# ScalarE's squares in the attention loop of a hybrid encoder layer: another place in the engine's order

## The chip, the cores and the metric

The kernel runs on one core of a Trainium2 chip. The metric is the device time of one execution in microseconds (us); three executions of the kernel before took 1003.96, 1005.08 and 1006.52 us, the median is 1005.08 us.

## The reference

One inference step of a one-layer hybrid encoder, all in f32, with 1024 prompt rows, 32 sample rows and a model width of 1024:

```
h = RMSNorm(x); z = h @ W_in          -> qA kA vA qB kB vB, heads of 64
mixer A: 8 query heads, 2 key heads, window of own chunk + 2 chunks of 64, sinks
mixer B: 8 heads, own chunk + 8 chunks, learned relative bias
x = x + W_out @ concat(RMSNorm_a(out_A), RMSNorm_b(out_B))
x = x + HierMoE(RMSNorm(x))           -> top 1 of 4 groups, then top 2 of 8 experts
```

Two norms matter here. RMSNorm_a and RMSNorm_b take the mean square over the 512 columns that each mixer gives for a row. The norm ahead of the mixture of experts takes the mean square over all 1024 columns of the row with its residual.

## The kernel before, in words

The rows lie in nine tiles of 128 (index t from 0 to 8; tile 7, `SAMPLE`, holds the sample rows, tile 8, `LAST`, the last prompt rows). There are three stages. The first (to about 295 us) projects and normalises all tiles. The second (to about 655 us) is the attention loop, with the output projection, the second norm and the router woven in. The third chooses experts and runs 24 steps over packed rows, with the expert weights streaming in from memory.

**The attention loop** is written out by hand for every engine: 75 iterations v, one pair of heads each (`units`; eight pairs to a tile, even v mixer A, odd v mixer B; iteration v = 8t + 2p + m). A unit u = 2v or 2v+1 is one head. Each engine runs its own list in this order, and semaphores tie the lists together:

- **TensorE** (line 1635 on): `transpose_probs(2v-2)` (L1499), `scores(v+1)` (L1484), `turn_rows(v)` (transposes of finished rows: L1623 for the mixers' outputs, L1534 for the second norm's), a piece of the output projection (`pe_pieces(2v)`, L1597; for tile 7 L1574 and L1581), `pair_back(v-3)` (L1529, which turns a pair's output back), `transpose_probs(2v-1)`, another piece, `values(v-2)` (L1516), router pieces (L1550, L1561). In iterations 1 to 14 `keep_busy` (L1384) adds matmuls whose result nobody reads; one f32 matmul shows as two records.
- **ScalarE** (L886 to L896): `pair_out(v-3)` (L808, copies the pair's output out of PSUM), `copy_pt(2v-2)` (L828, L831), `turned_out(v)` (L881), `probs(2v+2)` (L842, the exponents; L847 for the sinks of mixer A), `act_pieces(2v)`, `copy_pt(2v-1)`, `probs(2v+3)`, `act_pieces(2v+1)`, and at v = 10, 18, ..., 74 `squares_out(t)` with t = v // 8 - 1.
- **VectorE**: `copy_pt(2v-2)` (L1056), `biased(2v+2)` (L1140, adds mask or bias and takes the row minimum of the negated scores), pieces (`residual`, L1093; the second norm, L1118), `divide(v-3)` (L1068 to L1075), `copy_pt(2v-1)`, `biased(2v+3)`, at v = 11, 19, ... `norm_out(t)` (L1085), and router copies (L1102, L1107).

The names that the change and the prediction touch:

- `squares_out(t)` (L849) waits until all eight pairs of tile t are divided (`s_on`) and the norm of the tile before is made (`s_og`). It squares 512 columns twice (L854), and `rstd` (L722 Ln, L723 Exp) turns the two sums into reciprocal roots; `s_so` tells VectorE. `norm_out(t)` on VectorE waits for `s_so`, and `turn_rows` on TensorE, one iteration later for the first half of the row, waits for `s_og` of `norm_out`.
- `act_pieces(t, g)` (L859): at the step g = `squares` of a tile (given by `when(t)`) it waits for the residual (`s_x2`), squares 1024 columns (L867) and calls `rstd`; VectorE's second norm (L1118) waits for that. All these steps are odd, so they lie in `act_pieces(2v+1)`: v = 22, 30, 38, 46, 54, 61, 68 and 71 for tiles 0 to 7. For tile 7 at g = 11 and 13 (v = 69 and 70) it waits for the sample's part of the output projection (`s_pq`, L1574) and copies it out (L864).
- `probs(u)` waits for `biased(u)` (`s_sp`). TensorE transposes unit u one iteration or more later.
- `copy_pt` waits for the transposes of its unit; `turn_rows(v)` waits for ScalarE's `copy_pt(2v-2)`; `pair_back(v-3)` waits for `pair_out(v-3)`.
- SyncE loads experts 1 to 4 when the last pair is turned back (`s_ob`, set by L1529).

Of the kernel before, what the change touches and what calls it, by code (L numbers as in the profile page):

```python
# [59 lines left out]
SAMPLE, LAST = NT - 2, NT - 1  # L60
# [49 lines left out]
def build(nc, d, o):  # L110
    ctx = ExitStack()
    with ctx:
        def sem(name):
            return ctx.enter_context(nc.semaphore(name))
# [5 lines left out]
        def place(n, at=None):  # L120
            a = top[0] if at is None else at
            if at is None:
                top[0] += n
            assert a + n <= ARENA, (a, n)
            return arena[:, a:a + n]
# [20 lines left out]
        sso, rso = place(2), place(2)  # L146
# [25 lines left out]
        parts = xr[:, 1].rearrange("p (b c) -> p b c", b=2)  # L172
# [89 lines left out]
        def stored(e, c):  # L262
            at = weight_at(e, c)
            return arena[:, at:at + 512]
# [15 lines left out]
        def bank(n, a=0, b=512):  # L280
            return ps[:, n * 512 + a:n * 512 + b]
# [58 lines left out]
        s_on = sem("mixer_out_divided")  # L340
        s_so = sem("mixer_squares_summed")
        s_og = sem("mixer_out_normed")
# [82 lines left out]
        def unit_info(u):  # L425

            t, m, h = units[u]
            segs = tile_keys(TILE[t])[m]
            tiles, c = [], 0
            for col, n in segs:  # L430
                for k in range(0, n, P):
                    tiles.append((c + k, (col + k) // P, min(P, n - k)))
                c += n
            return t, m, h, segs, tiles, c

        def stat_at(m, h):

            return h // 4 * 8 + m * 4 + h % 4
# [38 lines left out]
        def pt_of(u):  # L477
            _, m, h = units[u]
            return (pt_a, pt_b)[m][:, h % 2]
# [8 lines left out]
        def pieces(do, u):  # L488

            for t in (u // 16 - 3, u // 16 - 2, u // 16 - 1):  # L490
                if 0 <= t < LAST:
                    do(t, u - 16 * (t + 1))
# [205 lines left out]
        def _(act):  # L698
# [17 lines left out]
            chain = Chain(act, s_act)  # L716
# [3 lines left out]
            def rstd(out, ms):  # L720

                chain.link(nc.scalar.activation(out, ms, ACT.Ln, bias=eps))  # L722
                return nc.scalar.activation(out, out, ACT.Exp, scale=-0.5)  # L723
# [86 lines left out]
            def copy_pt(u):  # L810

                if not 0 <= u < NU:
                    return
                _, _, _, _, tiles, _ = unit_info(u)
                cut = (len(tiles) + 1) // 2
                act.wait_ge(s_pt, u + 1)
                rest = tiles[cut:]
                if not rest:
                    act.sem_inc(s_pta, 1)
                    return  # L820
                if u >= 4:
                    act.wait_ge(s_pv[u % 2], u // 2 - 1)
                c0 = 0
                full = [x for x in rest if x[2] == P]
                ins = None
                if full:
                    c0 = len(full) * P
                    ins = nc.scalar.activation(pt_of(u)[:, cut * P:cut * P + c0], bank(5, 0, c0), ACT.Copy)  # L828
                if len(full) < len(rest):
                    n = rest[-1][2]  # L830
                    ins = nc.scalar.activation(pt_of(u)[0:n, cut * P + c0:cut * P + c0 + P], bank(5, c0, c0 + P)[0:n], ACT.Copy)  # L831
                ins.then_inc(s_pta, 1)

            def probs(u):

                if u >= NU:
                    return
                t, m, h, segs, tiles, width = unit_info(u)
                act.wait_ge(s_sp, u + 1)
                c = stat_at(m, h)  # L840
                shift = negm[:, t % 2, c:c + 1]
                nc.scalar.activation(sp[:, u % 4, 0:width], sp[:, u % 4, 0:width], ACT.Exp, scale=-1.0,  # L842
                                     bias=shift, accum_out=psum_e[:, t % 2, c:c + 1]).then_inc(s_p, 1)
                if m == 0:
                    if t >= 1:
                        act.wait_ge(s_on, u // 2 - 7)
                    nc.scalar.activation(esink[:, h:h + 1], sinks[:, h:h + 1], ACT.Exp, bias=shift).then_inc(s_es, 1)  # L847

            def squares_out(t):  # L849
                act.wait_ge(s_on, 8 * (t + 1))  # L850
                if t >= 1:
                    act.wait_ge(s_og, 2 * t)
                for m in range(2):
                    ins = nc.scalar.activation(junk[:, 512 * m:512 * m + 512], row[:, t, 512 * m:512 * m + 512], ACT.Square,  # L854
                                               scale=512 ** -0.5, accum_out=sso[:, m:m + 1])
                chain.link(ins)
                rstd(rso, sso).then_inc(s_so, 1)

            def act_pieces(t, g):  # L859
                if t == SAMPLE and g in (11, 13):  # L860
# [9 lines left out]
            def turned_out(v):  # L870

                turn = turn_of(v)
                if turn is None:
                    return
                kind, t, half = turn
                made, done = ((s_t1, s_ota), (s_t2, s_h2a))[kind]
                act.wait_ge(made, 2 * t + half + 1)
                if kind == 0 and half == 0 and t >= 2:
                    for r in range(2):
                        act.wait_ge(s_r[r], t - 1)  # L880
                nc.scalar.activation(turned[t % 2][:, 4 * half:4 * half + 4], bank(5).rearrange("p (g c) -> p g c", g=4),  # L881
                                     ACT.Copy).then_inc(done, 1)
# [3 lines left out]
            for v in range(NV + 3):  # L886
                pair_out(v - 3)
                copy_pt(2 * v - 2)
                turned_out(v)
                probs(2 * v + 2)  # L890
                pieces(act_pieces, 2 * v)
                copy_pt(2 * v - 1)
                probs(2 * v + 3)
                pieces(act_pieces, 2 * v + 1)
                if v % 8 == 2 and v >= 8:
                    squares_out(v // 8 - 1)  # L896
            def choice_exps(n):

                t0, t1 = ((0, EARLY), (EARLY, NT))[n]
# [3 lines left out]
            def second_exps(n):  # L903
# [2 lines left out]
                act.wait_ge(s_v12, n + 1)  # L906
                nc.scalar.activation(e12[:, t0:t1], e12[:, t0:t1], ACT.Exp).then_inc(s_v12e, 1)

            act.wait_ge(s_t1, 2 * LAST + 1)
            for r in range(2):  # L910
                act.wait_ge(s_r[r], LAST - 1)
# [462 lines left out]
        def _(pe):  # L1374
# [6 lines left out]
            def keep_busy(n, b=2):  # L1381

                for _ in range(n):
                    mm(bank(b, 0, P), ident, ident, start=True, stop=True)  # L1384
# [251 lines left out]
            for v in range(NV + 3):  # L1636
                if v == 1:
                    pe.wait_ge(s_tea, 2 + 2 * NT)
                    pe.wait_ge(s_tev, 2 + 2 * NT)
                transpose_probs(2 * v - 2)  # L1640
                scores(v + 1)
                turn_rows(v)
                pieces(pe_pieces, 2 * v)
                pair_back(v - 3)
                rows_turned(v)
                transpose_probs(2 * v - 1)
                pieces(pe_pieces, 2 * v + 1)
                values(v - 2)
                pieces(route_pieces, 2 * v)
                pieces(route_pieces, 2 * v + 1)  # L1650
                if 1 <= v < FIRST_OUT:
                    keep_busy(6 if v == 11 else 5 - v // 4, 6)
            turn_logits(SAMPLE)
            keep_busy(16)
            pe.wait_ge(s_og, 2 * NT)
# [1 line left out]
            for half in range(2):  # L1657
                for c in range(4):
                    k = 4 * half + c
                    ins = nc.tensor.transpose(bank(6 + half, c * P, c * P + P), row[:, LAST, k * P:k * P + P], ident)  # L1660
# [36 lines left out]
            for s in range(NT):  # L1697
                ins = mm(ps[:, NT * NE:NT * NE + NE], ones, mb[:, s], start=(s == 0), stop=(s == NT - 1))
# [3 lines left out]
            for n in range(4):  # L1702
                ins = mm(bank(1, 0, 2 * NSTEP), late_row[:, n], late_block[:, n].rearrange("p a c -> p (a c)"),
                         start=False, stop=(n == 3))
# [58 lines left out]
            for s in range(NSTEP):  # L1763
# [8 lines left out]
                if s == 22:  # L1772

                    pe.wait_ge(s_oin, 1)
                    for n in range(2 * NT):
                        ins = mm(bank(7, 0, 2 * NOVER), over_row[:, n], over_block[:, n].rearrange("p a c -> p (a c)"),
                                 start=(n == 0), stop=(n == 2 * NT - 1))
# [5 lines left out]
            with pe.If(nov > 0):  # L1783
                with pe.Fori(0, NOVER) as i:
                    with pe.If(i < nov):
                        pe.wait_ge(v_g, i * 16 + 16)
                        for g in range(8):
                            ins = nc.tensor.transpose(bank(2 + g // 4, g % 4 * P, g % 4 * P + P), xg[:, 0, g * P:g * P + P], ident)
# [4 lines left out]
                        for k in range(KD):  # L1793
                            ins = mm(bank(0), xgt[:, 0, k], stored(0, k * 512), start=(k == 0), stop=(k == KD - 1))
                        ins.then_inc(v_gu, 1)
                        pe.wait_ge(v_h, i + 1)
                        for f in range(2):
                            ins = nc.tensor.transpose(bank(4, f * P, f * P + P), hd[:, 0, f * P:f * P + P], ident)
# [4 lines left out]
                        for f in range(2):  # L1803
                            for n in range(2):
                                a = 2 * KD * FF + f * D + n * 512
                                ins = mm(bank(5 + n), hdt[:, 0, f], stored(0, a), start=(f == 0), stop=(f == 1))
# [100 lines left out]
```

## Time and profile before

| what | value |
|---|---|
| three executions, median (lowest, highest) | 1005.08 us (1003.96, 1006.52) |
| the profiled execution, its own time | 1007.59 us |
| span of its records | 1005.8 us |
| mean granted TensorE clock over the span | 0.987 |
| busy: TensorE, VectorE, ScalarE, GpSimd | 951.7, 375.1, 318.9, 88.3 us |

The profile's page gives busy time for each engine over the span and over 40 slices. The waits view adds up, for each line, how long its engine sat idle ahead of it and which line ended that. The timeline lists instructions in order of time with start, duration, engine, line, tiles, how many are merged, and in brackets the idle time before. The windows view gives busy time of all engines in a stretch with the granted TensorE clock (1.00 is full speed). PE is TensorE's matmul, PEld its weight load, DVE VectorE, ACT ScalarE, SP SyncE.

### The profile page before, as it was taken

To read this page: it belongs to the slowest core of one execution; us is meant where nothing else is said; L and a number is where in the kernel's file an instruction comes from. 1 tells how busy PE (TensorE), PEld (TensorE's weight loads), DVE (VectorE), ACT (ScalarE), POOL (GpSimd) and SP (SyncE) were. 2 spreads that over 40 slices of the span, in tenths; PEclk is the share of its full clock that TensorE was granted. 3 is DMA by queue.
4 is the path that set the end of the run, shared out by engine and by line. 5 is a ranking of instruction groups with operands and counts; after the bars stand their busy time and mean duration, and the time that the engine had idled before them with its cause. 6 is when DMAs were issued, how large, how long until landed. Compare 5 with 4: busy or idle time off the path is not lost. (4 is left out here: it accounts for less than half of the span.)

```text
span 1005.8 us, 16201 instructions
## 1 busy us (share of the span) xinstructions
PE 951.7 (95%) x6097; PEld 478.0 (48%) x6097; DVE 375.1 (37%) x1083; ACT 318.9 (32%) x937; POOL 88.3 (9%) x72
## 2 busy tenths in 40 slices
PE   6999999999989999999998998998999999999994
PEld 3454554455456545555555554568333333333341
DVE  0342334333365555555555445467311111111120
ACT  1211222122246555555556455411111111111110
POOL 1000000000030000000000000000122222222111
PEclk9999999999989999999999999899999999999998
DMA  8501111011057001101010140297899999999942
GB/s 342 214 27 41 42 42 42 0 42 42 1 209 259 1 22 43 64 1 64 1 64 22 43 189 22 85 387 305 318 370 390 390 379 393 391 393 386 375 121 29
DMA packets 35015, 164.64 MB, mean 164 GB/s; under 512 B 7872, under 2 KB 9952, under 8 KB 22016
## 3 DMA queue, kind: packets, MB, share of 16 engines
q1 hardware_dynamic: 24768, 134.92, 33.7%
q0 software_dynamic: 6912, 17.32, 6.9%
q10 hardware_dynamic: 3264, 11.44, 2.8%
q8 instruction: 47, 0.77, 0.3%
q14 instruction: 24, 0.20, 0.1%
HBM read 147.10 MB, written 24.41 MB: 171 GB/s over the span
## 5 line engine op out<-in xcount | busy, mean ns | idle before, releaser
L1397 PE MATMUL ps<-arena 128*128 128x512 f32 (+1 forms) x640 | 252.2, 554 | 8.6 <-DMA arena<-in_w_in 8.6
L1397 PEld LDWEIGHTS ps<-arena 128*128 128x128 f32 x640 | 121.4, 191 | 134.3 <-issue 129.5
L1730 PE MATMUL ps<-arena 128*32 128x512 f32 x1536 | 171.7, 598 | 0.8 <-ACT arena L931 0.8
L1597 PE MATMUL ps<-arena 128*128 128x512 f32 x224 | 114.7, 606 | 0.0
L842 ACT ACTIVATE arena<-arena 128x256 f32<-128x256 f32 (+6 forms) x144 | 83.8, 582 | 83.3 <-DVE arena L1140 82.0
L1730 PEld LDWEIGHTS ps<-arena 128*32 128x32 f32 x1536 | 47.8, 110 | 107.0 <-issue 105.9
L1140 DVE CUSTOM_DVE_ANT_0 arena<-ps,arena 128x256 f32<-128x256 f32 (+6 forms) x144 | 78.0, 543 | 31.2 <-PE ps L1484 30.8
L1748 PE MATMUL ps<-arena 128*32 128x512 f32 x768 | 87.0, 592 | 0.7 <-ACT arena L955 0.7
L1056 DVE COPY arena<-ps 128x128 f32<-128x128 f32 (+2 forms) x144 | 53.1, 369 | 63.1 <-PE ps L1499 62.6
L1499 PE MATMUL ps<-arena 128*128 128x128 f32 (+1 forms) x400 | 71.3, 283 | 4.0 <-ACT arena L881 1.6
L761 ACT ACTIVATE arena<-ps,arena 128x512 f32<-128x512 f32 (+1 forms) x36 | 24.8, 689 | 156.8 <-PE ps L1397 155.8
L1337 DVE SCALAR_TENSOR_TENSOR arena<-ps,arena 128x256 f32<-128x256 f32 x24 | 11.6, 485 | 165.8 <-ACT arena L947 165.8
L996 DVE TENSOR_TENSOR arena<-arena 128x640 f32<-128x640 f32 (+1 forms) x18 | 18.5, 1027 | 131.4 <-ACT arena L759 79.4
L1484 PE MATMUL ps<-arena 64*128 64x256 f32 (+4 forms) x384 | 62.4, 424 | 1.1 <-DVE arena L1140 1.1
L638 POOL DMA_INDIRECT arena<-h_rows,arena x24 | 25.1, 1047 | 423.6 <-DVE arena L1287 405.3
L1516 PEld LDWEIGHTS ps<-arena 128*64 128x64 f32 (+1 forms) x800 | 42.5, 136 | 40.8 <-DVE arena L1056 21.2
L1516 PE MATMUL ps<-arena 128*64 128x128 f32 (+1 forms) x800 | 61.2, 283 | 0.6 <-ACT arena L881 0.6
L947 ACT ACTIVATE arena<-ps 128x256 f32<-128x256 f32 x24 | 9.3, 387 | 160.2 <-PE ps L1730 160.2
L1499 PEld LDWEIGHTS ps<-arena 128*128 128x128 f32 (+1 forms) x400 | 43.7, 139 | 28.9 <-issue 16.0
L649 POOL DMA_INDIRECT out_y<-arena x24 | 38.0, 1584 | 215.6 <-issue 148.9
L1748 PEld LDWEIGHTS ps<-arena 128*32 128x32 f32 x768 | 25.1, 109 | 57.7 <-issue 56.8
L1384 PE MATMUL ps<-arena 128*128 128x128 f32 x324 | 43.1, 286 | 0.0
(170 smaller groups left out, 883.8 us busy)
## 6 DMA issues: line engine op xcount, KB each, us to landing
arena<-in_wexp SPq DMA_DIRECT2D x92, 1024.0 KB, 22.0
arena<-in_x SPq DMA_DIRECT2D x18, 512.0 KB, 4.3
arena<-in_w_in ACTq DMA_DIRECT2D x3, 2048.0 KB, 23.2
arena<-in_xT SPq DMA_DIRECT2D x9, 512.0 KB, 3.5
arena<-in_w_out SPq DMA_DIRECT2D x1, 4096.0 KB, 13.9
out_y<-arena SPq DMA_DIRECT2D x8, 512.0 KB, 2.7
h_rows<-arena SPq DMA_DIRECT2D x8, 512.0 KB, 2.9
arena<-in_wexp SPq DMA_DIRECT2D x8, 512.0 KB, 20.6
```

The source lines that it names most:

```text
L649: pool.indirect_dma_start(out=o["y"], out_offset=bass.IndirectOffsetOnAxis(ap=slot_token[:, s:s + 1], axis=0), in_=yb[:, (s + 1) % 2], in_ ...
L842: nc.scalar.activation(sp[:, u % 4, 0:width], sp[:, u % 4, 0:width], ACT.Exp, scale=-1.0, bias=shift, accum_out=psum_e[:, t % 2, c:c + 1]) ...
L1056: nc.vector.tensor_copy(pt_of(u)[:, 0:cut * P], bank(4, 0, cut * P)).then_inc(s_ptv, 1)
L1140: nc.vector.tensor_tensor_reduce(out=sp[:, u % 4, 0:width], in0=ps[:, at:at + width], in1=add, scale=-1.0, scalar=nsinks[:, h:h + 1] if m ...
L1384: mm(bank(b, 0, P), ident, ident, start=True, stop=True)
L1397: ins = mm(bank(Z_BANK[c], 0, CHUNK[c]), xt[:, j, k, :], w_in[:, a:a + CHUNK[c]], start=(k == 0), stop=(k == KD - 1))
L1484: ins = mm(ps[:, at:at + step], q, kt[:, col:col + step], start=True, stop=True)
L1499: ins = nc.tensor.transpose(dst[0:n], sp[:, u % 4, c:c + n], ident)
L1516: ins = mm(pv_ps[r * HD:(r + 1) * HD], kv, pt_of(2 * v + r)[0:n, i * P:i * P + P], start=(i == 0), stop=(i == len(tiles) - 1), tile_positi ...
L1597: ins = mm(bank(6), turned[t % 2][:, c], w_out[:, c, 512 * n:512 * n + 512], start=(c == 0), stop=(c == KD - 1))
L1730: ins = mm(bank(s % 2)[u:u + UNIT], xgt[:, s % 2, k, u:u + UNIT], stored(expert_of(s, q), k * 512), start=(k == 0), stop=(k == KD - 1), ti ...
L1748: ins = mm(bank(5 + n)[u:u + UNIT], hdt[:, s % 2, f, u:u + UNIT], stored(expert_of(s, q), a), start=(f == 0), stop=(f == 1), tile_position ...
```

## The change

`squares_out` gets a list of halves; the waits go with half 0, the reciprocal roots with half 1. For tiles 0 to 7 it leaves the end of iteration v = 8t + 10 and runs in iteration v = 8t + 11: half 0 ahead of `probs(2v+2)`, half 1 behind `copy_pt(2v-1)`. For tile 8 it stands after the loop, which is the place it had. `act_pieces(2v+1)` changes places with `probs(2v+3)` in every iteration. On TensorE, `keep_busy` at the end of iteration 11 makes 14 matmuls in place of 6.

```diff
-            def squares_out(t):
-                act.wait_ge(s_on, 8 * (t + 1))
-                if t >= 1:
-                    act.wait_ge(s_og, 2 * t)
-                for m in range(2):
+            def squares_out(t, parts):
+                if 0 in parts:
+                    act.wait_ge(s_on, 8 * (t + 1))
+                    if t >= 1:
+                        act.wait_ge(s_og, 2 * t)
+                for m in parts:
                     ins = nc.scalar.activation(junk[:, 512 * m:512 * m + 512], row[:, t, 512 * m:512 * m + 512], ACT.Square,
                                                scale=512 ** -0.5, accum_out=sso[:, m:m + 1])
-                chain.link(ins)
-                rstd(rso, sso).then_inc(s_so, 1)
+                if 1 in parts:
+                    chain.link(ins)
+                    rstd(rso, sso).then_inc(s_so, 1)
...
                 turned_out(v)
+                if v % 8 == 3 and v >= 8:
+                    squares_out(v // 8 - 1, (0,))
                 probs(2 * v + 2)
                 pieces(act_pieces, 2 * v)
                 copy_pt(2 * v - 1)
+                if v % 8 == 3 and v >= 8:
+                    squares_out(v // 8 - 1, (1,))
+                pieces(act_pieces, 2 * v + 1)
                 probs(2 * v + 3)
-                pieces(act_pieces, 2 * v + 1)
-                if v % 8 == 2 and v >= 8:
-                    squares_out(v // 8 - 1)
...
+            squares_out(LAST, (0, 1))
             act.wait_ge(s_t1, 2 * LAST + 1)
...
                 if 1 <= v < FIRST_OUT:
-                    keep_busy(6 if v == 11 else 5 - v // 4, 6)
+                    keep_busy(14 if v == 11 else 5 - v // 4, 6)
```

## Rows read from the trace of the kernel before

**Rows 1.** The page, busy time of each engine over the span

```profile
PE 951.7 (95%) x6097; PEld 478.0 (48%) x6097; DVE 375.1 (37%) x1083; ACT 318.9 (32%) x937; POOL 88.3 (9%) x72
```

**Rows 2.** Waits of TensorE from 320 to 655 us: total, times, longest (us)

```profile
PE ps L1529 <- ACT arena L808: 12.6, 14, 1.4
```

**Rows 3.** Timeline, iterations 34 to 36 (squares of tile 3): start, us, instruction

```profile
438.34 0.48 DVE L1140 CUSTOM_DVE_ANT_0 arena<-ps,arena 128x256 f32<-128x256 f32 x1
438.38 0.62 ACT L854 ACTIVATE arena<-arena 128x512 f32<-128x512 f32 x1
...
440.06 0.21 ACT L723 ACTIVATE arena<-arena 128x2 f32<-128x2 f32 x1
440.43 0.28 ACT L808 ACTIVATE arena<-ps 128x128 f32<-128x128 f32 x1 [0.16 <-issue]
...
440.76 0.33 PE L1529 MATMUL ps<-arena 128*128 128x128 f32 x1 [1.40 <-ACT arena L808]
...
441.46 0.28 ACT L828 ACTIVATE arena<-ps 128x128 f32<-128x128 f32 x1
...
442.37 1.41 DVE L1085 SCALAR_TENSOR_TENSOR arena<-arena 128x512 f32<-128x512 f32 x2
...
445.13 0.56 DVE L1056 COPY arena<-ps 128x384 f32<-128x384 f32 x1 [1.35 <-PE ps L1499]
```

**Rows 4.** Timeline, iterations 9 to 12 (squares of tile 0, keep_busy)

```profile
322.78 0.94 PE L1384 MATMUL ps<-arena 128*128 128x128 f32 x6
...
325.87 0.33 PE L1529 MATMUL ps<-arena 128*128 128x128 f32 x1 [1.30 <-ACT arena L808]
...
327.06 1.60 PE L1384 MATMUL ps<-arena 128*128 128x128 f32 x12
...
327.48 1.41 DVE L1085 SCALAR_TENSOR_TENSOR arena<-arena 128x512 f32<-128x512 f32 x2
...
329.44 0.66 PE L1623 MATMUL ps<-arena 128*128 128x128 f32 x4
```

**Rows 5.** Timeline, iterations 68 to 71 (residual squares of tile 6, sample's parts)

```profile
624.01 0.39 ACT L828 ACTIVATE arena<-ps 128x256 f32<-128x256 f32 x1
...
625.68 0.83 ACT L842 ACTIVATE arena<-arena 128x640 f32<-128x640 f32 x1 [1.28 <-DVE arena L1140]
...
626.51 1.04 ACT L867 ACTIVATE arena<-arena 128x1024 f32<-128x1024 f32 x1
...
628.00 0.20 ACT L723 ACTIVATE arena<-arena 128x1 f32<-128x1 f32 x1
...
628.60 1.11 PE L1623 MATMUL ps<-arena 128*128 128x128 f32 x4 [2.19 <-ACT arena L828]
...
631.02 3.64 PE L1574 MATMUL ps<-arena 128*32 128x512 f32 x16
...
640.38 1.93 PE L1574 MATMUL ps<-arena 128*32 128x512 f32 x16
...
641.97 0.83 ACT L842 ACTIVATE arena<-arena 128x640 f32<-128x640 f32 x1 [1.29 <-DVE arena L1140]
...
642.79 0.58 ACT L864 ACTIVATE arena<-ps 128x512 f32<-128x512 f32 x1
...
643.76 0.66 PE L1534 MATMUL ps<-arena 128*128 128x128 f32 x4 [0.49 <-ACT arena L828]
```

**Rows 6.** Windows: stretch, length, busy PE PEld DVE ACT POOL, PEclk, DMA share, GB/s

```profile
628.40:635.20 6.80, 6.13 (x29) 2.42 (x31) 2.25 (x7) 2.77 (x10) 0.00 (x0) 0.50 0.49 157
...
725.00:960.00 235.00, 235.00 (x2132) 81.97 (x2128) 37.47 (x60) 37.34 (x81) 51.68 (x39) 1.00 1.01 383
```

**Rows 7.** Timeline of SyncE's queue, 600 to 1005 us

```profile
654.25 288.83 SPq L562 DMA_DIRECT2D arena<-in_wexp  x97
```

**Rows 8.** Groups of ScalarE: count, busy us, mean ns, idle before

```profile
L717 ACT ACT_TABLE_LOAD x1 | 1.3, 1283 | 9.1 <-issue 9.1
L927 ACT ACT_TABLE_LOAD x1 | 1.3, 1283 | 0.0
```

## The prediction, made before the change was run

> **What bounds the kernel now.** I read the page first: TensorE is busy for 951.7 of 1005.8 us, ScalarE for 318.9 [rows 1]. So ScalarE's busy time as such can give nothing; the change moves work on ScalarE and can only pay where TensorE stands still for it. The waits view of the attention loop answers that: 14 times `pair_back` (L1529) found TensorE idle and was released by ScalarE's copy of the pair's output (L808), for 12.6 us in all [rows 2]. The timeline says which 14. Each time the copy stands right behind a set of squares: eight times behind those of the mixers' output (tiles 0 to 7), six times behind those of the residual row (tiles 0 to 5). The residual squares of tile 6 have their stall one line earlier, at the transposes of a finished row, and it is the longest of the loop, 2.19 us [rows 5].
>
> Tile 3 shows the pattern [rows 3]. ScalarE ends an exponent and at 438.38 begins two squares, logarithm and exponent, until 440.27 (440.06 + 0.21). Only then does the next iteration's L808 run, and L1529 starts after 1.40 us of idle TensorE. The squares are wanted by nobody so early: VectorE's norm (L1085) begins at 442.37, right behind its own earlier work, not behind the squares. The loop ends at 654.25, where SyncE, which waited for the last L1529, issues the expert weights [rows 7]. From 725 to 960 TensorE is busy without a gap and the DMA engines are full [rows 6], but both start from the loop's end, so what the loop saves should reach the end of the kernel.
>
> **The change, part by part.** No instruction of ScalarE is added or removed and no DMA is moved; SyncE's and GpSimd's queues are untouched.
>
> *Mixers' squares, tiles 1 to 7.* L808 and the copy behind it now run right after the exponent, so in tile 3 L808 would end near 438.7, before TensorE is ready for L1529 at 440.76 - 1.40 = 439.36: the stall goes whole. What is late next? Half 0 takes 0.62, and the exponent behind it, whose scores were ready at 438.82 (438.34 + 0.48), moves to about 439.4; its transposes come an iteration later. Half 1 stands behind the copy L828, which follows TensorE and so moves from 441.46 to about 440.06 and ends at 440.34. Half 1 with both small steps takes 0.62 + 0.65 (440.27 less 438.38 less two squares of 0.62): the roots are ready at about 441.6. VectorE's norm would be free to run at 442.37 - 1.40 = 440.97, so here is a new wait of 0.65 us. The norm then ends at 441.65 + 1.41 = 443.06. Queued behind it on VectorE is the copy L1056 of the next iteration, which waits for TensorE until 445.13 - 1.40 = 443.73. So 0.67 us of cover is left, and the new wait costs nothing; if the cover goes, every further tenth delays the next scores. The second exponent of the iteration, now behind the squares, starts about when it did; TensorE needs it an iteration later.
>
> *Residual squares, tiles 0 to 5.* They change places with an exponent that was waiting for VectorE anyway: at tile 6 the copy ahead ends at 624.40, and the exponent waits until 625.68, 1.28 us of idle ScalarE [rows 5]. The residual is added before that copy ends, so the added wait (`s_x2`), with the exponent and the whole next iteration queued behind it, should hold nothing. Squares and small steps take 628.20 - 626.51 = 1.69 us; 1.28 of that fills the idle time, 0.4 us pushes the exponent and L808. The six stalls were of the order of 1 us and L808 now comes 1.3 us earlier, so they go whole. The second norm on VectorE, which waited for these roots, gets them earlier too.
>
> The thirteen stalls of both kinds together: 12.6 - 1.30 (tile 0, next) = **11.3 us** gained.
>
> *Tile 0 and the fillers.* In iteration 11 the stall of 1.30 goes [rows 4]. Behind it stand 8 more filler matmuls, 16 records; 6 records take 0.94 and 12 take 1.60, so 0.11 each, **1.77 us** more. Next is L1623, the transposes of the row that VectorE's norm makes. The norm ended at 327.48 + 1.41 = 328.89; with the stall gone it could end 1.30 earlier, with a wait like tile 3's 0.65 later than that. With the fillers L1623 starts at 329.44 - 1.30 + 1.77 = 329.9, behind the norm in every case. So the fillers set the time and are not hidden: **0.47 us** lost. The bounds are 0.47 and, should they be hidden, a gain of 1.30.
>
> *Residual squares of tile 6.* L1623 waited for a copy behind L867 [rows 5]. With the squares ahead of the exponent that copy comes earlier by the 1.28 us of idle time that they fill, less some 0.2 for handing over between instructions (an estimate; one such gap is 0.16 in [rows 3]). So of 2.19 us about 1.1 stays: **1.1 us** gained; bounds 0.9 and 2.19.
>
> *The sample's parts.* `act_pieces` at v = 69 and 70 also hold L864, which waits for L1574, and an exponent is now queued behind it. At v = 69 the scores' copies come later than that exponent, no cost. At v = 70 L1574 ends at 642.31; L864 (0.58) and then the exponent (0.83) end near 643.8, where they ended at 643.37. Next is the copy that L1534 already waited 0.49 us for [rows 5]. **0.5 us** lost, bounds 0 and 0.83.
>
> *The clock.* From 628.4 to 635.2 the granted clock is 0.50, its 1.2 GHz level [rows 6]; TensorE had just stood idle for 2.19 us. L1574 takes 3.64 us there and 1.93 at 640.38 [rows 5], 1.71 more; L1623 takes 1.11 against 0.66 [rows 4], 0.45 more. That is 2.2 us at least; half of the 6.13 us busy in that stretch, 3.1, is the upper bound; nothing, if the clock falls all the same. Idle spells up to 1.40 us [rows 3] left the clock at full speed, and the 2.19 becomes 1.1. I take the step as gone, **2.6 us**, between the two bounds.
>
> **Sum.** -11.3 + 0.5 - 1.1 + 0.5 - 2.6 = **-14.0 us**. The profiled execution took 1007.59 us with a span of 1005.8, so its like would be 993.6. It lies 2.5 us over the median of the three runs; from that median I predict 1005.1 - 14.0 = **991.1 us**.
>
> **Rivals.**
> - *The clock still falls* there or at a neighbour: around 1.1 us of idle the transposes and their copies leave TensorE lightly loaded, which speaks for it; the calm at 1.40 us speaks against it. Then 991.1 + 2.6 = 993.7.
> - *VectorE's norm takes the place of ScalarE's squares.* The cover is 0.67 us in tile 3. If the roots came more than that later than I work out, the next scores would wait. Should all eight sites give back what they gain, the six residual stalls remain, at the mean of 12.6 / 14 = 0.9 each 5.4 us; with 1.1, 2.6, -0.5 and -1.8 for the fillers that is 6.8: 998.3. Against it: the terms are single rows of a regular loop.
> - *Hidden behind the experts.* If the weights' stream set the end from a fixed time, 1005. Against it: 97 loads are issued from 654.25 on, after the loop's last step.
> - *Slower: ScalarE reloads its tables.* Squares now stand between exponents at more places. If a square needed another table than the exponent, each of eight sites would gain one more switch there and one back, 16 loads of 1.283 us [rows 8] = 20.5 us on the engine that TensorE waits for; from 0.9 us a load on, the 14 us are eaten. 991.1 + 20.5 = 1011.6. Against it: the trace has only two loads, one at the start and one ahead of the experts [rows 8], though exponents, squares and logarithms alternate all through the loop. The Trainium skill (ScalarE: Activation LUTs, Table sets: the hidden batching unit) has the rule behind this: batch activations by table set, not by place. Its section What ACT_TABLE_LOAD costs puts a switch at 2.66 us, an estimate of 42.6 us here, 1033.7; the load alone agrees with the 1.283 us of the rows, and no switch in the loop shows.
>
> **How the numbers follow.** Forecast 0.64; clock falls 0.20; norm's wait 0.08; hidden 0.05; slower 0.03 (tables, or a stall I did not see). The ends: with the whole 2.19, 3.1 for the clock, no loss at the sample and none for the fillers the sum is -11.3 - 1.3 - 2.2 - 3.1 = -17.9, 987.2; upward the range reaches past the clock's and the norm's case to 998.5, leaving out the last two cases. Runs of this kernel tell 0.3%, 3 us, from no change. Faster by more: the first three cases, 0.92; within: 0.05; slower: 0.03.
>
> **What would show it.** L1529 behind L808: from 14 stalls to none or short ones. ScalarE's wait for L1140 ahead of the exponents shrinks. VectorE shows a new wait of some 0.6 us for L723 ahead of L1085, and L1056 behind it still waits for TensorE. L1384 in iteration 11 has 28 records, and L1623 follows them later than before by half a microsecond relative to the copy ahead. Near 617 us the clock stays at 1.00 and L1574 takes 1.93 twice. SyncE's L562 starts near 640. The prediction is wrong if L562 moves and the end doesn't, if L1623 or L1484 take over the stalls, or if a stretch at 0.50 stands elsewhere.

## The result, and the profile after the change

The kernel with the change took 988.5 us (median of four executions, 988.11 to 990.68), the kernel before beside it 1005.28 us (four, 1003.96 to 1006.52). The ratio is 0.9838, 95% interval 0.9818 to 0.9857: 16.8 us faster, where 14.0 was forecast (991.1, range 987.2 to 998.5). The profiled execution took 988.11 us with a span of 986.3. Measured once more beside nine other executions of the kernel before, the change gave 0.9818 (0.9805 to 0.9832; run a1_again, below).

Page of the kernel after: busy time by engine, to set against [rows 1].

```profile
PE 946.2 (96%) x6113; PEld 480.9 (49%) x6113; DVE 375.0 (38%) x1083; ACT 317.4 (32%) x937; POOL 88.2 (9%) x72
```

ScalarE is as busy as it was; TensorE has 16 records more (the eight fillers) and yet the span is 19.5 us shorter. Waits of TensorE in the attention loop (318 to 640 us), all whose total is 1.0 us or more: line that waited, line that released it, total, times, longest.

```profile
PE ps L1504 <- ACT arena L883: 1.7, 3, 0.6
PE ps L1489 <- DVE arena L1145: 1.1, 4, 0.3
PE ps L1504 <- DVE arena L1061: 1.1, 2, 0.5
PE ps L1539 <- ACT arena L828: 1.1, 1, 1.1
PE ps L1628 <- ACT arena L828: 1.0, 2, 0.8
```

The lines moved by 5 below the edit: `pair_back` L1529 is now L1534, the transposes L1623 and L1534 are L1628 and L1539, VectorE's norm L1085 is L1090. The row of [rows 2] (12.6 us, 14 times) is gone, and no row of its size has come in. SyncE's queue shows the end of the loop, 18.83 us earlier than in [rows 7]:

```profile
635.42 290.19 SPq L562 DMA_DIRECT2D arena<-in_wexp  x97
```

Timeline of the tile 3 site, the stretch of [rows 3]:

```profile
433.58 1.13 PE L1602 MATMUL ps<-arena 128*128 128x512 f32 x2
...
433.73 0.26 ACT L808 ACTIVATE arena<-ps 128x128 f32<-128x128 f32 x1
...
434.04 0.63 ACT L855 ACTIVATE arena<-arena 128x512 f32<-128x512 f32 x1
...
434.12 0.14 PEld L1534 LDWEIGHTS ps<-arena 128*128 128x128 f32 x1 [0.24 <-ACT arena L808]
...
434.55 0.27 PE L1534 MATMUL ps<-arena 128*128 128x128 f32 x1
...
434.66 0.38 PE L1504 MATMUL ps<-arena 128*128 128x128 f32 x2
...
435.49 0.62 ACT L855 ACTIVATE arena<-arena 128x512 f32<-128x512 f32 x1
...
436.56 0.21 ACT L723 ACTIVATE arena<-arena 128x2 f32<-128x2 f32 x1
...
436.81 1.42 DVE L1090 SCALAR_TENSOR_TENSOR arena<-arena 128x512 f32<-128x512 f32 x2 [0.75 <-ACT arena L723]
...
438.74 0.56 DVE L1061 COPY arena<-ps 128x384 f32<-128x384 f32 x1 [0.52 <-PE ps L1504]
...
439.91 0.42 PEld L1628 LDWEIGHTS ps<-arena 128*128 128x128 f32 x4
439.91 0.66 PE L1628 MATMUL ps<-arena 128*128 128x128 f32 x4
```

The copy of the pair's output (L808) now precedes the two halves of the squares (L855). Its consumer's weights are loaded at 434.12, while the matmul ahead still runs, and L1534 starts without idle time. The norm (L1090) waits 0.75 us for the roots; the copy queued behind it (L1061) still waits 0.52 us for TensorE, so that wait is covered. The norm ends at 436.81 + 1.42 = 438.23, and L1628, TensorE's transposes of the row that the norm makes, starts 1.68 us later without idle time. VectorE's wait for the roots, summed over the loop:

```profile
DVE arena L1090 <- ACT arena L723: 5.5, 8, 1.0
```

These are eight waits of 0.5 to 1.0 us, one for each of tiles 0 to 7, and TensorE's list above has no wait for the norm (L1090). The wait of the second norm for its roots (8.8 us, 7 times before) is gone. Next come two stretches of TensorE: iterations 11 and 12 [rows 4] with 28 filler records, and tile 6 with the sample's parts [rows 5].

```profile
325.66 3.39 PE L1389 MATMUL ps<-arena 128*128 128x128 f32 x28
...
329.84 0.66 PE L1628 MATMUL ps<-arena 128*128 128x128 f32 x4
...
611.88 0.66 PE L1628 MATMUL ps<-arena 128*128 128x128 f32 x4 [0.78 <-ACT arena L828]
...
613.60 1.93 PE L1579 MATMUL ps<-arena 128*32 128x512 f32 x16
...
620.98 1.92 PE L1579 MATMUL ps<-arena 128*32 128x512 f32 x16
...
624.93 0.66 PE L1539 MATMUL ps<-arena 128*128 128x128 f32 x4 [1.07 <-ACT arena L828]
```

The stall of tile 6 fell from 2.19 to 0.78 us and the two passes of the sample's projection take 1.93 and 1.92. The sample's later stall grew from 0.49 to 1.07. The window from 600 us to the loop's end has the full clock, where [rows 6] had 0.50:

```profile
600.00:640.00 40.00, 34.44 (x300) 22.24 (x297) 21.42 (x63) 22.33 (x66) 0.00 (x0) 1.00 0.27 97
```

**Where the time came from.** The start of each `pair_back` in the kernel before, taken from its start after, tells how much earlier (minus) or later the kernel with the change is there. The table shows by how much this difference grows in each stretch. Worked out from the two traces' rows (us):

```
up to iteration 10                              +0.10
iteration 11  stall of tile 0                   -1.38   (reported idle 1.30)
iteration 12  fillers                           +1.66   forecast of both: +0.47, found +0.28
12 to 68      13 stalls                        -15.54   forecast -11.3
66            (no stall reported there)         -0.16
69, 70        tile 6 and the half clock         -4.09   forecast -1.1 - 2.6 = -3.7
71            sample's parts                    +0.58   forecast +0.5
sum                                            -18.83
one site (tile 3): iteration 35 -1.56, iteration 36 -0.18; reported idle 1.40
```

### The profile page after: what moved, and what is told of

The parts are those of the page before. It is cut to its first block and busy times, and to the rows that moved or that the text cites. A ratio compares the mean times of both kernels' runs of the same rounds, so it can differ in the third digit from the quotient of the medians.

```text
span 986.3 us, 16233 instructions
## 1 busy us (share of the span) xinstructions
PE 946.2 (96%) x6113; PEld 480.9 (49%) x6113; DVE 375.0 (38%) x1083; ACT 317.4 (32%) x937; POOL 88.2 (9%) x72
## 5 line engine op out<-in xcount | busy, mean ns | idle before, releaser
L1602 PE MATMUL ps<-arena 128*128 128x512 f32 x224 | 114.7, 606 | 0.0
L1061 DVE COPY arena<-ps 128x128 f32<-128x128 f32 (+2 forms) x144 | 53.1, 368 | 57.3 <-PE ps L1504 56.9
L1504 PE MATMUL ps<-arena 128*128 128x128 f32 (+1 forms) x400 | 70.6, 281 | 4.1 <-ACT arena L883 1.7
L1489 PE MATMUL ps<-arena 64*128 64x256 f32 (+4 forms) x384 | 62.4, 424 | 1.1 <-DVE arena L1145 1.1
L1504 PEld LDWEIGHTS ps<-arena 128*128 128x128 f32 (+1 forms) x400 | 44.2, 139 | 30.3 <-issue 18.5
L1389 PE MATMUL ps<-arena 128*128 128x128 f32 x340 | 46.5, 292 | 0.0
```

Of the source, the lines that this page charges most:

```text
L1061: nc.vector.tensor_copy(pt_of(u)[:, 0:cut * P], bank(4, 0, cut * P)).then_inc(s_ptv, 1)
L1489: ins = mm(ps[:, at:at + step], q, kt[:, col:col + step], start=True, stop=True)
L1504: ins = nc.tensor.transpose(dst[0:n], sp[:, u % 4, c:c + n], ident)
L1602: ins = mm(bank(6), turned[t % 2][:, c], w_out[:, c, 512 * n:512 * n + 512], start=(c == 0), stop=(c == KD - 1))
```

## The experiments

The theory (A in most expectations): TensorE lost what ScalarE's squares put between an exponent and the copies behind it; each stall is worth more than its reported idle time; the longest one also halved the clock. Rivals: the stalls are worth only their idle time (B, and the rest came from the clock or from chance); only one of the two moves matters; the halves, the fillers or the cover behind VectorE's norm are what makes it work.

**e1_mixers: the mixers' squares alone.** The swap of the residual squares is undone.

```diff
-                pieces(act_pieces, 2 * v + 1)
                 probs(2 * v + 3)
+                pieces(act_pieces, 2 * v + 1)
```

> The mixers' squares moved in halves, with 14 fillers in iteration 11; the residual squares stay behind the exponent. Theory A (a stall of TensorE costs its reported idle time and about 0.34 us more, because the instructions behind it start with nothing loaded ahead): seven sites 5.98 + 7 x 0.34 = 8.4 us gained, fillers 0.3 lost, so SyncE's expert loads start at 654.25 - 8.1 = 646.1; the half-clock stretch behind iteration 68 stays. Time about 997.2. Theory B (a stall costs its reported idle time, and the rest of what the changed kernel gained has another source, such as VectorE's later norm): 5.98 - 0.3 = 5.7 us, loads at 648.5, time about 999.6.

Measured: 998.15 us (996.7 to 999.1, four executions), ratio 0.9925 (0.9909 to 0.9942); the loads begin at 646.25. Waits and timeline of TensorE, and a window (length, busy PE, PEld, DVE, ACT, POOL, granted clock, DMA share, GB/s):

```profile
PE ps L1534 <- ACT arena L808: 5.3, 6, 1.1
...
621.13 1.11 PE L1628 MATMUL ps<-arena 128*128 128x128 f32 x4 [2.19 <-ACT arena L828]
...
619.70:626.50 6.80, 4.89 (x23) 1.82 (x23) 2.41 (x7) 3.65 (x14) 0.00 (x0) 0.50 0.43 154
```

Six stalls are back, and with the 2.19 us of tile 6 so is the stretch at half clock. The mixers' sites step as in the kernel after (tile 3: -1.56 and -0.18), so the two moves are independent. In this execution the clock was also halved for 3.4 us at 544.6 us, 0.4 us after the 1.03 us stall of iteration 55, and `pair_back` lost 1.69 there; the kernel after shows nothing there.

**e2_residual: the residual squares alone.** The kernel before, with the swap only.

```diff
-                probs(2 * v + 3)
                 pieces(act_pieces, 2 * v + 1)
+                probs(2 * v + 3)
```

> The residual squares change places with the exponent, the mixers' squares stay where they were, 6 fillers in iteration 11. Theory A: six sites 5.32 + 6 x 0.34 = 7.4 us, tile 6 and the clock 4.1, the sample's parts 0.6 lost: loads start at 654.25 - 10.9 = 643.4, no half-clock stretch near 620, time about 994.4. Theory B: 5.3 + 3.7 - 0.5 = 8.5 us, loads at 645.7, time about 996.8. If the clock falls for another reason than the 2.19 us stall, the stretch at 0.50 stays and each is 2.6 us longer.

Measured: 997.07 us (996.79 to 997.93, four), ratio 0.9922 (0.9906 to 0.9939); the loads begin at 642.17, with a loop that began 2.98 earlier and lost 1.59 to a stretch at half clock at 324.3. Waits and timeline of TensorE, and a window over tile 6:

```profile
PE ps L1529 <- ACT arena L808: 7.3, 8, 1.4
...
618.63 0.66 PE L1623 MATMUL ps<-arena 128*128 128x128 f32 x4 [0.78 <-ACT arena L828]
...
612.00:640.00 28.00, 23.77 (x202) 14.55 (x201) 16.00 (x47) 15.99 (x44) 0.00 (x0) 1.00 0.25 91
```

The mixers' eight stalls are left and the six others are gone. Their steps are again the idle time plus about a third of a microsecond, but for the site of iteration 31, which gives its 1.12 us and only 0.17 more, as in the kernel after. The stall of tile 6 is 0.78 and the clock stays at 1.00. The two parts of the change gain 6.8 and 7.9 us in their medians, together 14.7, where the whole change gained 16.8 and, measured again, 18.3. The medians hold what the clock did in each execution; the loop alone can be told from the profiles. In them the loop, from the first to the last `pair_back`, is 350.5 us before, 343.4 in e1 and 341.4 in e2; less the 1.69 and 1.59 of the stretches at half clock that only they have, that is 8.8 and 10.7 gained, together 19.5 where the whole change gains 18.9. So the parts add up to within 0.6 us in the loop.

**e3_fillers6: six fillers as before, with the rest of the change.**

```diff
-                    keep_busy(14 if v == 11 else 5 - v // 4, 6)
+                    keep_busy(6 if v == 11 else 5 - v // 4, 6)
```

> The changed kernel with 6 fillers in iteration 11 in place of 14. Theory A: the eight fillers set the time there, the row transposes of iteration 12 come 0.9 us earlier (then VectorE's norm, which ends at 328.8, holds them): time about 987.6, loads at 634.5, clock at 1.00 all through the attention loop. Rival: the fillers keep the clock up while TensorE waits for the norm; without them a stretch at 0.50 shows between 325 and 345 us and the time is 989 to 991.

Measured: 987.36 us (984.94 to 989.91, four), ratio 0.9831 (0.9812 to 0.985), not to be told from the kernel after. The trace is finer: iteration 12 loses 0.75 in place of 1.66, and the clock stays at 1.00 through the whole loop.

```profile
327.75 0.63 PE L1628 MATMUL ps<-arena 128*128 128x128 f32 x4 [0.83 <-DVE arena L1090]
```

So the eight fillers hide a wait for VectorE's norm and cost 0.9 us more than that wait. In this execution they were not needed for the clock. They have one more effect: the 0.16 us at iteration 66 in the table above shows, as 0.14 or 0.15, in every profile with 14 fillers (also e1, e4, e5, e6, a1_again) and in none with six (both repeats of the kernel before, e2, e3, e7). How fillers 55 iterations ahead do that stays open.

**e4_whole: both halves and the roots at the first place.**

```diff
-                    squares_out(v // 8 - 1, (0,))
+                    squares_out(v // 8 - 1, (0, 1))
...
-                if v % 8 == 3 and v >= 8:
-                    squares_out(v // 8 - 1, (1,))
```

> The changed kernel with both halves and the roots at the first place, ahead of the exponent of 2v+2. Theory: the copy behind that exponent (copy_pt of 2v-1) comes 1.3 us later and TensorE's values wait for it at all eight sites, about 1.8 us at tile 0 and 0.5 at each other: 5 us lost, time about 993.5; VectorE's wait for the roots ahead of its norm goes. Rival: the halves do not matter, since the copy has 1.3 us to spare: time 988.5 as the changed kernel.

Measured: 988.45 us (986.77 to 989.9, four), ratio 0.9834 (0.9817 to 0.9851), and the loads begin at 635.40, 0.02 from the kernel after. My theory of a 5 us loss fell, the rival held. VectorE at tile 3:

```profile
435.95 1.41 DVE L1088 SCALAR_TENSOR_TENSOR arena<-arena 128x512 f32<-128x512 f32 x2
...
438.71 0.56 DVE L1059 COPY arena<-ps 128x384 f32<-128x384 f32 x1 [1.35 <-PE ps L1502]
```

The norm no longer waits, and the copy behind it has 1.35 us of cover again, as in [rows 3]. What is pushed back (the exponent and the second copy) is wanted by TensorE only in the next iteration, by the order of the lists. The split into halves gains nothing.

**b1_before, b2_before: the kernel before, unchanged, two more profiles.**

> The kernel before, unchanged, for another profile. If the 2.19 us stall behind iteration 68 brings the clock down whenever it occurs, a stretch at 0.50 of 6.8 us shows right behind it (near 628 us less whatever the start differs) and L1574 takes 3.6 us at its first pass. If the stretch was chance, L1574 takes 1.93 us both times and the clock stays at 1.00 from 300 to 650 us; the span is then about 2.6 us shorter than the 1005.8 shown.

> The same as b1_before, once more: does the stretch at 0.50 behind iteration 68 come every time or by chance?

Timeline of TensorE and a window, first b1_before:

```profile
625.83 1.12 PE L1623 MATMUL ps<-arena 128*128 128x128 f32 x4 [2.18 <-ACT arena L828]
...
624.40:631.20 6.80, 4.89 (x23) 1.82 (x23) 2.41 (x7) 3.65 (x14) 0.00 (x0) 0.50 0.45 157
```

then b2_before:

```profile
626.29 0.66 PE L1623 MATMUL ps<-arena 128*128 128x128 f32 x4 [2.18 <-ACT arena L828]
...
628.00 3.49 PE L1574 MATMUL ps<-arena 128*32 128x512 f32 x16
...
628.20:631.60 3.40, 3.40 (x18) 0.61 (x12) 0.89 (x4) 1.00 (x5) 0.00 (x0) 0.50 0.82 292
```

They took 1004.17 and 1003.98 us, one execution each. The 2.18 us stall is there each time, and each time the clock drops to 0.50 at it: during the idle time in one, 1.9 us after it in the other, for 6.8 and 3.4 us. With the first profile and e1_mixers that makes four of four profiles that have this stall. In the kernel after, its repeat, e2, e3, e4, e6 and e7 the stall is 0.8 us or less and no stretch at 0.50 lies near tile 6; in e5, with the same short stall at 625.03 us, one does (626.8). The stretch does not cost the same each time: the step from each of these profiles to the kernel after at iterations 69 and 70, less the 1.4 us by which the stall shrinks, leaves 2.7 us for the first profile, about 2.15 for b1 and e1, and 1.6 for b2. Near 290 us, ahead of the loop, the halved clock comes in some profiles and not in others, of both kernels: the first profile of the kernel before and that of the kernel after had it for 6.8 us (first `pair_back` at 303.4 and 303.5), b1 and b2 did not (300.7 and 301.1).

**e5_price: the price of a stall.** The kernel after with two squares of 1024 columns, whose result nobody reads, ahead of `pair_out` at v = 11, 19, ..., 67.

```diff
             for v in range(NV + 3):
+                if v % 8 == 3 and 8 <= v < 72:
+                    for _ in range(2):
+                        chain.link(nc.scalar.activation(junk, row[:, v // 8 - 1], ACT.Square, scale=D ** -0.5))
                 pair_out(v - 3)
```

> The changed kernel with two squares of 1024 columns, whose result nobody reads, ahead of pair_out in the eight iterations v = 11, 19, ..., 67: about 2.4 us of ScalarE time in the place that the mixers' squares left, where they took 1.89. Theory A: the stalls come back with about 0.5 us more idle time each, 11.3 us reported, and cost 0.34 more each: loads start at 635.4 + 14 = 649.4, and TensorE's L1534 moves at each site by its reported idle plus 0.34. Theory B: the move is the reported idle, loads at 646.7.

Measured: 1003.61 us (one execution); the loads begin at 650.26. Waits of TensorE in the loop, and the tile 3 site:

```profile
PE ps L1537 <- ACT arena L808: 10.1, 8, 1.7
...
441.90 0.14 PEld L1537 LDWEIGHTS ps<-arena 128*128 128x128 f32 x1 [2.34 <-ACT arena L808]
...
441.90 0.33 PE L1537 MATMUL ps<-arena 128*128 128x128 f32 x1 [1.51 <-ACT arena L808]
```

Eight stalls were put back, 10.1 us by their idle time. Against the kernel after, tile 3's site moves by 1.68 and the next iteration by another 0.18, 1.86 for a reported 1.51. All eight moves come to 12.6: 0.32 to 0.35 over the idle time at each but the first, 2.5 us in all, where A expected 2.7 more than B. That difference decides, and not the load time: less idle time came back than either theory had put in (10.1 for 11.3), the loop began 1.2 earlier, and two stretches at half clock (326.4 and 626.8) cost 1.75 and 1.69; 635.42 + 12.6 - 1.2 + 3.4 is 650.2.

**e6_late_roots: the cover behind the norm.** The kernel after with three squares of 512 columns, which nobody reads, ahead of half 1.

```diff
                 copy_pt(2 * v - 1)
+                if v % 8 == 3 and 8 <= v < 72:
+                    for _ in range(3):
+                        chain.link(nc.scalar.activation(junk[:, 512:], row[:, v // 8 - 1, 512:], ACT.Square, scale=512 ** -0.5))
                 if v % 8 == 3 and v >= 8:
```

> The changed kernel with three squares of 512 columns, whose result nobody reads, between copy_pt of 2v-1 and half 1 at the same eight iterations: the roots come about 2.3 us later, L808 of the iteration is untouched. Theory: VectorE's norm then ends behind TensorE's transposes of the row, which wait for it, and ScalarE's next copies are late too; the cover of half a microsecond is used up and each site loses about 0.8 us: loads start near 641, time near 994. Rival: the cover is larger and nothing is lost: loads at 635.4.

Measured: 989.67 us (one execution); the loads begin at 638.33, with a loop that began 3.05 earlier, so the loop is 5.96 us longer. VectorE and TensorE at tile 3, and the wait over the loop:

```profile
439.06 1.42 DVE L1093 SCALAR_TENSOR_TENSOR arena<-arena 128x512 f32<-128x512 f32 x2 [2.73 <-ACT arena L723]
...
440.39 0.55 DVE L1064 COPY arena<-ps 128x384 f32<-128x384 f32 x1
...
440.63 0.63 PE L1631 MATMUL ps<-arena 128*128 128x128 f32 x4 [0.38 <-DVE arena L1093]
...
PE ps L1631 <- DVE arena L1093: 5.4, 7, 1.4
```

Roots later by about 2 us (2.73 against 0.75) bring stalls back through VectorE's norm: the cover is finite. Which wait sets it is not the one that the prediction named. At tile 3 the copy behind the norm (L1064) no longer waits for TensorE, so its cover of 0.52 us is used up and more, yet TensorE loses only 0.42 of the 2 us, and loses it at L1631, the transposes of the row that the norm makes. In the kernel after these start 1.68 us after the norm's end at tile 3, and 0.69 (tile 1) to 1.93 (tile 7) at the other sites. Seven sites lose from 0.42 to 1.42, the least covered one most; tile 7, where L1631 does not wait, loses 0.17. These seven stalls cost hardly more than their idle time: 5.67 us for a reported 5.4, 0.04 over it at each. The time of this one execution stayed low although the loop is longer: it had the full clock ahead of the loop, where the kernel after had 0.50 for 6.8 us, and its loop began 3.05 earlier. The loop's length is what counts here.

**a1_again and e7_best: what is left.** a1_again is the kernel after, unchanged. e7_best has six fillers, the residual squares of tile 6 one piece later, and the sample's copies behind the exponent again.

```diff
-                return dict(adds=(17, 24), squares=25, norm=26, turns=(4, 5, 14, 15), router=31, logits=33)
+                return dict(adds=(17, 24), squares=26, norm=27, turns=(4, 5, 14, 15), router=31, logits=33)
...
                 probs(2 * v + 3)
+                pieces(sample_part, 2 * v + 1)
...
-                    keep_busy(14 if v == 11 else 5 - v // 4, 6)
+                    keep_busy(6 if v == 11 else 5 - v // 4, 6)
```

> The changed kernel once more, as the yardstick of the next run. 988.5 us (988.1 to 990.7) by every theory; the last pair is turned back and the expert loads start near 635.4 us.

> The changed kernel with 6 fillers in iteration 11 in place of 14, the residual squares of tile 6 one piece later (and their norm with them), and the sample's copies (L864) behind the exponent again. Theory A (what is left of the loop's losses is these three terms): 0.9 for the fillers, 0.6 for the sample's exponent, 0.78 + 0.34 = 1.1 for the stall of tile 6, so the loads start near 632.8 us and the time falls to about 986. Theory B (the squares of tile 6 lie on a chain that VectorE's norm and the router close): the stall moves to the transposes of that norm's row one iteration later, only the 0.9 and the 0.6 are gained, loads near 633.9. Theory C (without the sample's copies early, or with 6 fillers, TensorE's clock falls somewhere in the loop): no gain or a loss of 2 us, with a stretch at 0.50 between 300 and 635 us.

Measured: a1_again 987.64 us (987.14 to 988.22, five), ratio 0.9818 (0.9805 to 0.9832); e7_best 985.1 us (984.47 to 987.81, five), ratio 0.9799 (0.9782 to 0.9816). The intervals overlap, so e7 is probably, not surely, the faster. e7's timeline of ScalarE and TensorE at tile 6 and the sample, and SyncE's queue:

```profile
607.92 0.83 ACT L842 ACTIVATE arena<-arena 128x640 f32<-128x640 f32 x1 [1.29 <-DVE arena L1148]
...
609.23 0.66 PE L1631 MATMUL ps<-arena 128*128 128x128 f32 x4 [0.58 <-ACT arena L828]
...
621.70 0.66 PE L1542 MATMUL ps<-arena 128*128 128x128 f32 x4 [0.49 <-ACT arena L828]
...
632.19 290.22 SPq L562 DMA_DIRECT2D arena<-in_wexp  x97
```

From a1_again to e7_best the iterations step by -0.92 at 12, +0.16 at 66, -0.19 at 69 and -0.59 at 71: 1.54, against theory B's 1.5 and theory A's 2.6. (The rest of the 3.2 us in the load time is an earlier start.) B's number is right, its mechanism is not: the stall of tile 6 did not move to another row. It stays at 0.58, with no squares ahead of the copy any more, because the exponent there waits 1.29 us for VectorE's scores. What the squares still cost there in the kernel after is thus 0.2 us. The 0.16 at iteration 66 goes with the six fillers, as in e3.

## Why the prediction was right, point by point

**The mechanism held.** All 13 stalls went whole, the norm's new wait came as worked out (0.65 forecast for tile 3, 0.75 found; the copy's wait behind it 0.67 forecast, 0.52 found), and the gain reached the end: the loads begin 18.83 us earlier and the span is 19.5 shorter. e1 and e2 show that each move takes away its own stalls and no others.

**One term was mis-sized: the thirteen stalls, 11.3 us in the prediction, 15.5 found.** The step "12.6 - 1.30 = 11.3" took the reported idle time as the price. Found is 0.33 us more at a stall, (15.54 - 11.3) / 13: 0.32 to 0.35 at twelve of them and 0.17 at one. It has two parts, which the tile 3 site shows. First, idle time is counted from the end that the profile gives to the matmul ahead; in the kernel after, L1602 ends by its record at 433.58 + 1.13 = 434.71, yet L1534 starts at 434.55. A stream without stalls overlaps those ends by 0.16 us. The Trainium skill (Perfetto Trace Analysis, Tensor Engine Instruction (MATMUL, LD_WEIGHTS)) says that TensorE's reported ends are estimated from the size of the instruction; the overlap agrees. Second, after a stall the next weights are not loaded ahead: in e5 the load of L1537's weights starts with its matmul (441.90), in the kernel after 0.43 us ahead of it, and the instructions behind a stall follow 0.18 us later. No run tried the late load alone, but the site with 0.17 speaks for it (tile 1, iteration 31, in the kernel after):

```profile
414.10 0.14 PEld L1534 LDWEIGHTS ps<-arena 128*128 128x128 f32 x1 [0.65 <-ACT arena L808]
...
414.11 0.32 PE L1534 MATMUL ps<-arena 128*128 128x128 f32 x1
...
414.36 0.41 PE L1504 MATMUL ps<-arena 128*128 128x128 f32 x2
```

Here the idle time went, but L808 still comes so late that the weights are loaded only with the matmul. L1504 follows 0.25 us behind L1534, where it follows 0.11 behind at tile 3 (434.66 after 434.55). So the 0.18 goes with the late load there, and not with idle time.

That a stall of `pair_back` costs about a third of a microsecond more than its idle time is shown in both directions, by taking stalls away (the change, e1, e2) and by putting them back (e5). It does not hold for every stall of TensorE. The stalls of the row transposes in e6 cost 0.04 more, and the rows fit the same two parts: the record of the matmul ahead of them (L1489 in the kernel after) overlaps their start by only 0.07 us without a stall, and their weights are loaded with the first matmul (439.91, both) even so, so a stall can lose no early load there.

**Tile 6 and the clock: 1.1 + 2.6 in the prediction, 4.09 found.** The stall fell by 2.19 - 0.78 = 1.41, inside the bounds of 0.9 and 2.19; the other 2.68 is what the clock gave back, against 2.6. That these two agree so well holds for the one profiled execution: by the other profiles with the long stall the clock gives back 1.6 to 2.2. The rival that the clock still falls did not come true: with the long stall the stretch at 0.50 came in four profiles of four, without it in one of eight (e5). One argument against that rival was weaker than it looked, namely that idle spells up to 1.40 us leave the clock at full speed. They did in that trace, but a stretch at 0.50 began 0.4 to 1.8 us after a stall of 1.03 (e1), 1.31 (e2), 1.70 and 0.78 us (e5), while in the kernel before's three profiles the stalls at the same places as those of 1.03 and 1.31 left it at 1.00.

**Tile 0 and the sample.** Tile 0 and the fillers together lost 0.28 us, where 0.47 was forecast, and the sample's parts 0.58, where 0.5 was forecast. The fillers set the time in iteration 12, as forecast; e3 shows that they cover a 0.83 us wait for the norm.

**The other rivals.** The norm's wait is present and covered, and e6 shows that it would have cost some 6 us with roots 2 us later. The prediction's step "if the cover goes, every further tenth delays the next scores" held only in part: in e6 tile 3 has roots some 1.4 us beyond that cover, and TensorE loses 0.42, at the row's transposes and not at the scores. The gain was not hidden behind the experts: the loads moved and so did the end. Tables were not reloaded: the trace still has two table loads of 1283 ns, at the start and ahead of the experts, as in [rows 8]; so these squares stand between exponents at no such price. One sign of being wrong did show, a stretch at 0.50 elsewhere: the kernel after has one of 3.4 us at 669.8, behind the loop, where the kernel before has none. It is no effect of the change alone, since a1_again, the same kernel, has none there.

**From the profile to the median.** By the two traces the loop gains 18.9 us, 4.9 more than the sum of 14.0; the medians differ by 16.8 and, measured again, 18.3. So the forecast came nearer to the result than its sum deserved, and that part is luck. The kernel before's profiled execution was longer than all four executions of the result and had the halved clock twice by the loop's end; it was 2.3 us over their median. From the first to the last `pair_back` its three profiles took 350.5, 349.9 and 349.6 us; the kernel after, a1_again and e4 took 331.6, 331.7 and 331.5. The loop's gain is thus 18 to 19 us, and no trace shows where the medians lose the rest; that the clock's changes from execution to execution are behind it is argued, not shown.

## What to carry to other kernels

When one engine bounds and another feeds it through a strict order, look at the waits of the bounding engine, not at the feeder's busy share: moving 1.9 us of ScalarE's work behind the copy that TensorE wanted removed eight stalls without removing an instruction. Place slack work right after a handover. Follow its result to the bounding engine and take as cover the time that it lies ready there (0.69 to 1.93 us between the norm's end and L1628 here), and not only the wait of the next instruction on the way (0.67 us). The work need not be split finer than that consumer asks (e4). When a stall is priced by its reported idle time, look at two things in a place without the stall: by how much the record ahead overlaps the next start, and whether the next weights are loaded ahead. Here they made 0.33 us more at `pair_back` and 0.04 at the row transposes. And look behind each of the longest stalls for a halved clock.

## What was not expected of the hardware

A stall of `pair_back` on TensorE cost a third of a microsecond more than its idle time, nearly alike for stalls of 0.2 to 1.5 us (0.17 at one site), while a stall at the row transposes cost 0.04 more. One idle spell of 2.18 us in the loop was met by a halved granted clock in four profiles of four, for 3.4 or 6.8 us and at a loss of 1.6 to 2.7 us, while shorter spells, up to 1.7 us, left it at 1.00 nearly everywhere (not at 544.6 in e1, 324.3 in e2, 326.4 and 626.8 in e5). Some stretches at 0.50 (near 290, 325, 545, 627 and 670 us) come in some executions of a kernel and not in others, so that two profiles of one kernel differ by 2 to 3 us ahead of the loop alone; lengths between two instructions of one loop are a finer measure than start or end times.
